# A decoder step with 64 experts: where the last experts' rows are added, and how the two copies of the sums are joined

## The reference

```python
eidx = top_k(masked scores, 8)                  # 8 of 64 experts for each token
hb = silu(xb @ exp_gate[e]) * (xb @ exp_up[e])  # 1024 -> 256, for the tokens of expert e
yb = (hb @ exp_down[e]) * g[:, None]            # 256 -> 1024, times the token's weight
routed = segment_sum(yb, token)                 # add the 8 rows of each token
x = layer_norm(ALPHA * x + shared + routed, ln2_g, ln2_b)
```

## Time and profile before

| what | value |
|---|---|
| median of 3 runs | 1083.47 us (1079.4 to 1086.22) |
| profiled execution | 1083.88 us, its span 1081.8 us |
| mean granted TensorE clock | 0.961 |
| busy: TensorE, VectorE, ScalarE, GpSimd | 95%, 66%, 21%, 30% |
| DMA | 282.64 MB, mean 261 GB/s; 380 to 390 GB/s while the experts run |

### The profile page before, as it was taken

One profiled execution on the slowest core, in us unless ns is written; L12 is line 12 of the kernel. 1 busy time (PEld: TensorE's weight loads), 2 busy tenths in 40 slices (PEclk: granted clock), 3 DMA queues, 4 the chain that ended last, 5 costly groups with the idle time before them and its releaser, 6 DMA issues.

```text
span 1081.8 us, 31303 instructions
## 1 busy us (share of the span) xinstructions
PE 1026.4 (95%) x13698; PEld 741.5 (69%) x13699; DVE 710.3 (66%) x1547; ACT 228.2 (21%) x480; POOL 327.6 (30%) x330
## 2 busy tenths in 40 slices
PE   8999999878889999999999999999999999999976
PEld 6877888665754458687767777777777777777742
DVE  0789869888876696975578555556555655565326
ACT  2145612122446312101111111011111111111114
POOL 2000010000000001445555455554455555555411
PEclk9999999878859999999999999999999999999997
DMA  7221222250066429599999999999999999999962
GB/s 227 78 60 39 59 60 84 43 163 3 7 205 241 171 83 373 194 356 382 389 390 389 378 384 390 385 386 387 388 385 395 392 387 387 389 389 376 353 197 107
DMA packets 92038, 282.64 MB, mean 261 GB/s; under 512 B 22552, under 2 KB 49689, under 8 KB 67061
## 3 DMA queue, kind: packets, MB, share of 16 engines
q1 hardware_dynamic: 74685, 243.55, 58.1%
q0 software_dynamic: 16272, 33.84, 12.2%
q10 hardware_dynamic: 944, 3.24, 0.8%
HBM read 260.93 MB, written 36.25 MB: 275 GB/s over the span
## 4 chain that ended last, share of the span: by engine, by line
PE 68%; DVE 8%; ACT 2%; DMA 1%; issue 1%; POOLq 0%; DVEq 0%; SPq 0%; ACTq 0%
PE ph L2378 32%; PE ph L2406 21%; PE ph L1542 3%; PE ph L1560 2%; DVE w_exp L176 1%; PE pz_late L1583 1%; PE ph L1683 1%; DMA scr_f<-arena,row 1%; PE pt L1475 1%; PE pz_late L1500 1%; PE pt L2539 1%; PE pz_late L1501 0%; PE pst L1455 0%; PE pt L1478 0%; PE pt L933 0%
## 5 line engine op out<-in xcount | busy, mean ns | idle before, releaser
L2378 PEld LDWEIGHTS ph<-arena,w_exp 128*64 128x64 f32 x8192 | 342.0, 139 | 51.3 <-issue 47.5
L2378 PE MATMUL ph<-arena,w_exp 128*64 128x96 f32 x8192 | 353.9, 248 | 2.1 <-DVE arena L2363 2.1
L2406 PE MATMUL ph<-w_exp,arena 128*96 128x512 f32 x512 | 235.1, 602 | 1.2 <-DVE arena L2396 1.2
L977 POOL DMA_INDIRECT x_area<-scr_x,piece_row x192 | 203.0, 1057 | 82.9 <-issue 54.7
L2433 POOL DMA_INDIRECT scr_f<-arena,row x63 | 93.9, 1490 | 215.1 <-PE ph L2378 166.7
L523 PE MATMUL pz<-w_exp 128*128 128x260 f32 x672 | 155.7, 389 | 0.3 <-ACT w_exp L335 0.3
L2406 PEld LDWEIGHTS ph<-w_exp,arena 128*96 128x96 f32 x512 | 78.4, 163 | 110.2 <-issue 102.1
L523 PEld LDWEIGHTS pz<-w_exp 128*128 128x128 f32 x672 | 128.0, 193 | 22.4 <-issue 2.7
L2424 DVE TENSOR_SCALAR arena<-ph,row_weight 96x512 f32<-96x512 f32 x64 | 47.8, 747 | 138.6 <-PE ph L2406 138.6
L2363 DVE STREAM_TRANSPOSE arena<-x_area 128x768 f32<-128x768 f32 x64 | 104.2, 1628 | 5.3 <-DMA x_area<-scr_x,piece_row 4.6
L2387 ACT ACTIVATE arena<-ph 128x192 f32<-128x192 f32 x64 | 21.1, 330 | 409.6 <-PE ph L2378 402.6
(11 more groups left out here) (394 smaller groups left out, 1025.4 us busy)
## 6 DMA issues: line engine op xcount, KB each, us to landing
w_exp<-in_exp_up_dram SPq DMA_DIRECT2D x64, 1024.0 KB, 23.9
w_exp<-in_exp_down_dram SPq DMA_DIRECT2D x64, 1024.0 KB, 24.4
w_exp<-in_exp_gate_dram SPq DMA_DIRECT2D x64, 1024.0 KB, 21.8
w_exp<-in_w_in_dram SPq DMA_DIRECT2D x22, 512.0 KB, 3.7
w_exp<-in_x_prompt_dram SPq DMA_DIRECT2D x8, 512.0 KB, 5.4
w_exp<-in_w_out_dram SPq DMA_DIRECT2D x2, 2048.0 KB, 11.6
w_exp<-scr_f SPq DMA_DIRECT2D x8, 512.0 KB, 5.8
x_area<-scr_x,piece_row POOLq DMA_INDIRECT x192, 7.6
```

What stands on the lines that cost most here:

```text
L977: nc.gpsimd.indirect_dma_start(m.x_pieces[:, s, r, :], None, m.scr_x1.rearrange("t (q c) -> (t q) c", q=QUADS), bass.IndirectOffsetOnAxis( ...
L2378: last = nc.tensor.matmul(pgu[64 * half:64 * half + 64, s % 2, (2 * part + j) * CAP:(2 * part + j + 1) * CAP], w[job.slot][:, k, f0:P * ha ...
L2406: last = nc.tensor.matmul(pyl[0:CAP, c, :], hid[:, s % 2, j, :], m.expert_down[job.slot][:, j, c * 512:(c + 1) * 512], start=(j == 0), sto ...
```

## The change

- Experts 58 to 61 (`ONE_COPY` = 58) are all scattered into copy 0, each behind the landing of the one before. `wait_added` translates an expert's number into the semaphore and count of its landing.
- Copy 1 is complete with expert 57. SP loads it behind scatter 57 and the down product of 58 (the sample tile behind that of 59), into slot 4, whose weights have been used; copy 0 is loaded behind scatter 61, into slot 5.
- VectorE joins all five tiles itself: 0 and 1 ahead of the weighting of expert 62, 2 and 3 ahead of that of 63, the sample tile behind it. GpSimd joins nothing.
- Expert 62 is not scattered either. Its rows and those of 63 are added by TensorE with two one-hot tiles (`sum_of`), and VectorE adds that sum out of PSUM to the joined tile (`add_sum`), with the mean out of the same instruction's accumulator (for the sample tile, ScalarE still takes the mean). The identity products go.
- On TensorE the down product of 61 comes ahead of gate and up of 62; then gate and up of 62 and of 63, down of 62, down of 63. Activations and gate products on ScalarE and VectorE follow that order.
- `ORDER` is 0, 1, sample, 2, 3.
- The extra jobs are adapted to the same scheme; none runs.

```diff
+    ONE_COPY = E - 6
...
+    def copy_of(q):
+        return q % 2 if q < ONE_COPY else 0
+
+    def wait_added(eng, q):
+        count = q // 2 + 1 if q < ONE_COPY else ONE_COPY // 2 + q - ONE_COPY + 1
+        eng.wait_ge(added[copy_of(q)], 16 * count)
...
         if job.has_before(2):
-            act.wait_ge(added[s % 2], 16 * job.pair)
+            wait_added(act, q - 2)
... (weigh_dve likewise)
     def add_rows(pool, job):
...
-            pool.wait_ge(added[s % 2], 16 * job.pair)
+            wait_added(pool, q - 2 if q <= ONE_COPY else q - 1)
...
     def sync(sp):
...
-        sp.wait_ge(added[1], 16 * (E // 2 - 1))
-        for i in ORDER:
+        wait_added(sp, ONE_COPY - 1)
+        sp.wait_ge(y_done, 2 * (E - 5))
+        for i in range(TM):
             t0, n = TOK_TILES[i]
-            sp.dma_start(f_odd[i][0:n, :], m.scr_f[1][t0:t0 + n, :]).then_inc(odd_loaded[i], 16)
-        each_job(sp, body)
-        sp.wait_ge(gu_done, E)
-        sp.wait_ge(added[0], 16 * (E // 2))
-        sp.wait_ge(overflow_over, 1)
-        for i in ORDER:
+            sp.dma_start(f_odd[i][0:n, :], m.scr_f[1][t0:t0 + n, :]).then_inc(odd_loaded, 16)
+        sp.wait_ge(y_done, 2 * (E - 4))
+        sp.dma_start(f_odd[TM][0:B, :], m.scr_f[1][T:TT, :]).then_inc(odd_loaded, 16)
+        wait_added(sp, LAST - 2)
+        for i in range(NT):
             t0, n = TOK_TILES[i]
             sp.dma_start(f[i][0:n, :], m.scr_f[0][t0:t0 + n, :]).then_inc(f_loaded[i], 16)
...
     def tensor(pe):
-            if q + 1 < E:
-                gate_up(pe, Job(q + 1), (0, 1) if q + 2 < E else (0,))
+            if q + 1 < LAST - 1:
+                gate_up(pe, Job(q + 1))
+            if q == LAST - 1:
+                gate_up(pe, Job(q))
+                gate_up(pe, Job(LAST))
...
             down(pe, Job(q))
...
+        pe.wait_ge(one_hot_ready, 2)
+        for c in range(2):
+            sum_of(LAST - 1, 0, c)
+        pe.wait_ge(y_act, E)
+        sum_of(LAST, 0, 0)
+        pe.wait_ge(y_dve, E)
+        sum_of(LAST, 0, 1).then_inc(f_summed, 1)
+        for i in ORDER[1:]:
+            if i == 2:
+                pe.wait_ge(overflow_over, 1)
+            if i == 3:
+                pe.wait_ge(sums_added, 1)
             for c in range(2):
+                sum_of(LAST - 1, i, c)
+                last = sum_of(LAST, i, c)
+            last.then_inc(f_summed, 1)
...
     def vector(dve):
+        def join(i):
+            n = TOK_TILES[i][1]
+            dve.wait_ge(odd_loaded, 16 * NT)
+            dve.wait_ge(f_loaded[i], 16)
+            ch.link(nc.vector.tensor_tensor(f[i][0:n, :], f[i][0:n, :], f_odd[i][0:n, :], ALU.add))
+
+        def add_sum(at, i):
+            dve.wait_ge(f_summed, at + 1)
+            if i < TM:
+                ch.link(nc.vector.scalar_tensor_tensor(f[i], f_sum[i], 1.0, f[i], ALU.mult, ALU.add, accum_out=aggr[:, i, 0:1]))
+                nc.vector.tensor_scalar(aggr[:, i, 0:1], aggr[:, i, 0:1], 1.0 / D, None, ALU.mult).then_inc(sums_added, 1)
...
+            if q == LAST - 1:
+                gate_mul(dve, Job(q))
+                gate_mul(dve, Job(LAST))
+                for i in (0, 1):
+                    join(i)
+            if q == LAST:
+                for i in (2, 3):
+                    join(i)
+            weigh_dve(dve, Job(q))
             if q == LAST - 2:
                 dve.wait_ge(tokens_ready, 1)
-                nc.vector.tensor_scalar(of_last, of_last, row_weight[0:CAP, Job(LAST).l, 0:1], None, ALU.is_equal).then_inc(of_last_ready, 1)
-            weigh_dve(dve, Job(q))
+                dve.wait_ge(x_ready, E)
+                for of in (LAST - 1, LAST):
+                    nc.vector.tensor_scalar(one_hot[of], tokens, row_weight[0:CAP, Job(of).l, 0:1], None, ALU.is_equal).then_inc(one_hot_ready, 1)
...
+        join(TM)
         each_job(dve, body)
+        add_sum(0, 0)
         dve.wait_ge(ln2_loaded, 32)
+        scale_row(0, 0)
+        for at, i in enumerate(ORDER):
+            if at + 1 < NT:
+                add_sum(at + 1, ORDER[at + 1])
+            shift_row(at, i)
+            if at + 1 < NT:
+                scale_row(at + 1, ORDER[at + 1])
...
     def gpsimd(pool):
-        for q in range(E - AHEAD - 1, LAST):
+        for q in range(E - AHEAD - 1, LAST - 1):
             add_rows(pool, Job(q))
```

More of the change, by code:

```diff
@@ L2322, in each_job, with root, sum_of @@
                     body(k, ex)
[L2324 to L2333, removed]
     def squares(act, i):
         n = TOK_TILES[i][1]
-        nc.scalar.activation(f_unused[i][0:n, 1, :], summed(i), ACT.Square, scale=-1.0, bias=aggr[0:n, i, 0:1],
+        nc.scalar.activation(f_unused[i][0:n, 1, :], f[i][0:n, :], ACT.Square, scale=-1.0, bias=aggr[0:n, i, 0:1],
                              accum_out=aggr[0:n, i, 1:2]).then_inc(square_ready, 1)
-    def scale_row(dve, i):
+    def root(act, at, i):
         n = TOK_TILES[i][1]
[L2342 to L2356, removed]
+        act.wait_ge(square_ready, at + 1)
+        nc.scalar.activation(aggr[0:n, i, 2:3], aggr[0:n, i, 1:2], ACT.Sqrt, scale=1.0 / D, bias=m.eps_ln[0:n, :]).then_inc(rooted, 1)
+    def sum_of(q, i, c):
+        t0, n = TOK_TILES[i]
+        out = f_sum[i][:, c * 512:(c + 1) * 512] if i < TM else sample_sum[c][0:n, :]
+        return nc.tensor.matmul(out, one_hot[q][:, t0:t0 + n], y_rows[q][:, c * 512:(c + 1) * 512],
+                                start=(q == LAST - 1), stop=(q == LAST))
     def turn_pieces(dve, job):
@@ L2370, in gate_up @@
             pe.wait_ge(hid_ready, q - 1)
-        for part in parts:
+        for part in range(2):
             w = (m.expert_gate, m.expert_up)[part]
@@ L2380, in gate_up @@
                                                 start=(k == 0), stop=(k == KD - 1))
-        if 1 in parts:
-            last.then_inc(gu_done, 1)
+        last.then_inc(gu_done, 1)
     def gate_act(act, job):
@@ L2536, in add_joined @@
[L2536 to L2550, removed]
@@ L2551, in tensor @@
-        for i in (1, 2):
-            add_last(i)
-            pe.wait_ge(joined_dve, i + 1)
-            add_joined(i).then_inc(f_summed, 1)
-        pe.wait_ge(square_ready, 1)
-        pe.wait_ge(scaled, 1)
-        add_last(3)
-        pe.wait_ge(joined_pool, 2)
-        add_joined(3).then_inc(f_summed, 1)
+            pe.wait_ge(o_of_ready, k + 1)
+            pe.wait_ge(o_y_ready, k + 1)
+            for i in range(NT):
+                t0, n = TOK_TILES[i]
+                if i > 0:
+                    pe.wait_ge(o_added, NT * k + i)
+                for c in range(2):
+                    last = nc.tensor.matmul(pyl[0:n, c, :], o_of[:, t0:t0 + n], o_y_list[:, c * 512:(c + 1) * 512], start=True, stop=True)
+                last.then_inc(o_summed, 1)
@@ L2641, in body @@
             dve.wait_ge(o_y_done, k + 1)
-            for b in range(2):
-                dve.wait_ge(added[b], 16 * (E // 2 - b))
             for c in range(2):
```

160 lines of the change are left out of this document (68 added, 92 removed).

## The result

The changed kernel takes 1086.81 us in the median of 18 runs (1083.51 to 1089.06), the kernel before 1082.9 us beside it (1078.19 to 1086.22): a ratio of 1.003, 95% interval 1.0018 to 1.0043, or 2 to 5 us more. The forecast was 1088 us, 0.4% more. The change is a small loss here. The loss is not the same everywhere: in a later group of runs, in which TensorE needed 10 us per expert instead of 9, the same kernel was 0.8% faster than before.

A forecast was written before the change was run, and what follows sets the result against it. TensorE makes up 68% of the last chain, DMA near full rate beside it until about 1022 us; L 1045.0 + tail 41.1 = span 1086.1, 4.3 us later, so median 1083.5 + 4.3 = 1088 us; range 1080 to 1094.

The forecast's parts named there:

- L: Landing of the last scatter the final loads wait for: forecast 1045.0 us, bounds 1041.5 to 1051.2; before 1048.9.
- The starts behind a landing: Gap between one scatter's landing and the next one's start in copy 0: 0.8 us each, three times.
- Scatters 58, 59 and 61: Scatter-adds in series into copy 0: 9.8, 9.8 and 4.5 us to landing.
- scatter 60: Third scatter in series: 6.4 us, the middle of 4.5 and 8.2, since copy 1's loads may still run.
- The hold: Down 63's second half waits for weight 62, queued behind two VectorE joins: TensorE stands idle for 9 us.
- The clock: TensorE at 1.2 instead of 2.4 GHz from L + 7.7 to L + 13.4, costing 3.5 us before the first tile's sum.
- The tail: From L to the span's end: 15.9 + 22.2 + 3.0 = 41.1 us; before 32.9, VectorE becoming the bound.
- tile 0's sum: TensorE's four matmuls of the first tile: done at L + 15.9, before at L + 11.1.
- the accumulator's read: Extra step of VectorE's add that takes the mean: 0.2 us per tile, bounds 0 and 0.7.
- Parts costed at nothing: Down 61 ahead of gate and up 62 on TensorE: rows come 5.4 us earlier, then wait for scatters; nothing won.
- Down 61's weights: Weights for the moved down product: landed at 1022.1, wanted at 1023.8, so in time by 1.7 us.

The follow-up runs named there:

- a2: Changed kernel with only experts 60 and 61 scattered into one copy (`ONE_COPY = E - 4`), 10-us condition: ratio 0.9926 to the kernel before.
- d3: d1 with VectorE's order weight 62, joins 0 and 1, weight 63, joins 2 and 3, sample: ratio 1.0028 to the kernel before.
- d4: Changed kernel with the VectorE order of d3 and no late scatter, 9-us condition: ratio 1.0023 to the kernel before.
- d1: Changed kernel with GpSimd issuing scatter 61 only after the first half of down 62, a wait already over: ratio 1.0048 to the kernel before.
- d2: d1 with eight unread filler matmuls of 512 columns between the halves of the down product of 63: ratio 1.0067 to the kernel before.
- a3: Changed kernel with the down product of 61 put back behind gate and up of 62, 10-us condition: ratio 0.9945 to the kernel before.
- c1: The changed kernel itself, run again in the 10-us condition: ratio 0.9923 to the kernel before.

## Why the prediction was right

The direction, the size and most steps hold. L came 1.5 us later than forecast and the tail behind it was 2.9 us shorter; that the sum is so near is in part luck, since the two errors have opposite signs.

**L.** Forecast 32.9 us behind the start of scatter 58, measured 34.4. The starts behind a landing took 0.9 to 1.0 us each instead of 0.8. Scatters 58, 59 and 61 took 9.6, 9.3 and 4.55, forecast 9.8, 9.8 and 4.5. The term that was mis-sized is scatter 60: 8.1 us, where I took the middle of two rows, 6.4. It had the same length as the row for a scatter beside copy 1's loads, 8.1. The Trainium skill, "DMA: Bandwidth & Descriptors", section on queues, rings and completion order, says that a DMA engine takes turns between the queues that have work; by that the forecast put it at 8.2. The trace agrees as far as it goes: DMA moved 238 GB/s from 1030 to 1033, beside the start of scatter 60, and 87 from 1035 to 1038. Which queue's packets it shared the engines with is not shown. That the scatters in series set L in the 9-us condition is read from the chain; it was not tested there by an edit, since a2 ran in the other condition.

**The hold.** VectorE's joins ahead of the weighting of 62 and a TensorE gap of about 9 us: measured 9.6, in the place forecast. d3 and d4 show by experiment that this order costs 3 us of tail in the 9-us condition (35.4 and 35.3 us against 38.2, 38.6 and 38.6), one profile each.

**The clock.** The half clock was there, until 4.8 us behind the new start instead of 5.7. The rows at either level give 1.8 us for the second half (3.73 against 1.93) and 0.6 for the sums of tile 0 (4.24 against 3.60; 1.0 in d1, which took 4.59). That the path would be shorter by as much at full clock was only argued: d2 did not isolate it.

**The tail.** Forecast 41.1 us, measured 38.2. Up to tile 0's sum 14.7 instead of 15.9, since the second tile landed earlier (both joins took 2.58 us in one piece) and the clock came back sooner. Behind it 23.5 instead of 25.2: the accumulator's read takes 0.08 us instead of 0.2, and VectorE's instructions follow each other every 1.20 us although each is 1.28 long, over some ten of them. VectorE had no gap of more than 0.7 us there.

**Parts costed at nothing.** Down 61's weights were in time. That the step is worth nothing is read from the chain for the 9-us condition; in the 10-us one a3 shows 1.8 to 2.8 us of L.

**What I did not see** is how much hangs on where L lies against TensorE's last products. The change takes the last scatter and GpSimd's join off the end, and pays by scatters in series and by more work in VectorE's queue. Take the time from G to the end, less the down products that are left behind G: before 39.8 - 3.6 = 36.2 us in the 9-us condition, c1 34.2 - 7.1 = 27.1 in the 10-us one, the changed kernel in the 9-us one 46.8 - 7.1 = 39.7. By this, some 9 us are won where L comes early (the 0.8% of c1), and 3.5 us are lost where it comes late. There is no profile of the kernel before in the 10-us condition, so the 36.2 is carried over. And only the small step of a3 tests a later L without a change of condition: with L 2.8 us later against G than in c1, the end is 4.4 us later and the gap is back. That L alone makes the whole difference between the conditions is argued, not shown, since scatters, loads and TensorE's pace differ between them too.

## What to carry to other kernels

Before an instruction that waits for a load is put ahead of one that frees a buffer for another engine, find out how late the load can be: the order that was free when loads landed ahead cost 3 us when they landed 8 us behind. Price a transfer in a series by the row with the same traffic beside it, not by the middle of two. And know on which side of a balance a change works: this one gained 0.8% in one group of runs and lost 0.3% in another, with the kernel before measured beside it in both.

## What the runs showed of the hardware

- The same kernel took 1153 to 1154 us in two groups and 1082 in the third. In the slower condition the gate and up products of an expert take 6.5 us instead of 5.4, with gaps of 0.3 to 0.4 us that end for nothing the profile shows ("issue"), while the granted clock is 1.0. The up weights land 10.7 us behind their issue (34.4 in the other), although DMA's share is 1.0 in both, at 365 GB/s against 386 (600 to 700 us, c1 and the changed kernel). The last two pairs of products, with DMA at a share of 0.3 to 0.5, take the 5.4 us of the faster condition. The cause stays open.
- A scatter-add of 96 rows of 4 KB took 9.3 to 9.6 us in the changed kernel with DMA at a share of 0.9 to 1.0, 8.1 at 0.53 and 4.5 when nearly alone.
- VectorE's accumulator read is an instruction of its own of 0.08 us, and an add from PSUM with an accumulator takes 1.22 us for 128x1024, no more than one without (1.28).
- The filler of d2, which ended 2.5 us ahead of the second half, did not keep the clock up for it: the clock fell 2.6 us behind its last matmul. It fell 1.9 us behind the last one in the kernel before and about 4.1 in the changed kernel (1041.1 to 1045.2). In a3 an idle time of 2.7 us was enough: the clock fell 0.6 us after TensorE had begun again.
